# A two-layer and two-mixer block on one core: GpSimd's low parts of the weights in four operations instead of one

## The chip, the core and the metric

The kernel runs on one core of a Trainium2 chip. The metric is the device time of one execution in microseconds; several executions are timed, and the median counts.

## What is computed

The reference runs two models one after the other on a sequence of 512 tokens of width 1024, in float32. The first has two transformer layers with a context of 256 tokens (so 768 tokens in its first layer), the second two mixer layers. Cut to the matrix products and what stands between them:

```python
# first block, layer 0 (neighborhood attention) and layer 1 (sliding window attention)
u = modulate(rms_norm(h, g_mix), shift, scale)
q, k, v = split(u @ wqkv); y = attention(rms_norm(q), rms_norm(k), v) @ wo
h = h + gate * y
h = h + gate2 * (square(relu(modulate(rms_norm(h, g_mlp), shift2, scale2) @ w1)) @ w2)
# second block, layer 0: differential attention and mLSTM side by side; layer 1: gated spatial mixer
y = concat(diff_attention(hn @ w_in), mlstm_chunkwise(hn @ w_in)) @ w_out
h = h + rmsnorm(y, post_g)
y = (gelu(u) * (w_spatial @ rmsnorm(gelu(v))) * silu(z)) @ w_out     # u, v, z = hn @ w_in
h = h + rmsnorm(y, post_g)
```

## The kernel before

Every large product is made in three passes. A float32 operand is written as a high part, rounded to the matmul's fp32r format, and a low part, the rest. `mm3` (lines 274 to 278) issues three matmuls for each tile: high by high, low by high, high by low. So all weights must be split too. They stream from HBM in chunks of 128 partitions x 2048 columns into two slots of `w_raw` (m.raw). For each chunk, in a fixed order of chunks:

- SyncE issues the load once both parts of the chunk that had the slot before are made.
- ScalarE copies `w_raw` to `w_hi` (`split_hi`, line 239, or a line of the stage), once TensorE has used the slot's old high part.
- GpSimd subtracts: `w_lo` = `w_raw` - `w_hi`. It waits for ScalarE's count, makes one tensor_tensor of 2048 columns, and raises the count on which TensorE and SyncE wait. This is `split_lo` (line 242) in the MLP stages, and a line of the stage's own in the others: L1209 in the first attention stage, L1802 in the second, L2382 and L2385 in the differential attention, L2880 and L2883 in the mLSTM, L3495 in the last mixer.
- TensorE waits for the low part before the first matmul on the chunk.

The stages follow each other, each a block with its own program on every engine: first attention (`na_stage`), MLP, second attention (`swa_stage`), MLP, differential attention (`diff_stage`), mLSTM, last mixer (`odd_stage`). Each engine works through a fixed list of instructions; the waits between the lists are semaphore counts, and nothing is reordered at run time.

What VectorE does between the products matters here. At the start of a stage it makes the normalized input `u_lo`, in pairs of instructions per 128 channels: a scaling (L463) and a subtraction (L472, or L470 where there is no shift), with ScalarE's `u_hi` between them; TensorE waits for each 128 channels. In the attention stages it makes the softmax of one unit (a pair of heads or a head, and a block of queries) while TensorE scores the next one and works through projections. In `swa_stage` that is `maximum` (reductions L1952 and L1955, then L1960, a tiny operation on `stat`), the exponentials on ScalarE (L1846, L1849), and `normalise` (L1967 to L1973), whose `e` TensorE transposes (L2160). In `diff_stage` it is `maximum` (L2525, L2529), the exponentials (L2430), and `combine` (L2535 to L2540), whose `e` goes to TensorE at L2706; `low_y` (L2564) makes the low part of the attention's output between two such units. In `na_stage` the maxima end in L1364 and `e` is made in L1377 for TensorE's L1566.

GpSimd has one other kind of work: five additions of squares for each of six norms (L356).

Of the kernel before, what the change touches and what calls it, by code (L numbers as in the profile page):

```python
# [7 lines left out]
ALU = mybir.AluOpType  # L8
ACT = mybir.ActivationFunctionType
F32 = mybir.dt.float32  # L10
# [6 lines left out]
LAT = 512  # L17
# [10 lines left out]
CHUNK = 2048  # L28
# [212 lines left out]

def split_lo(pool, m, c, s, width=CHUNK):
    pool.wait_ge(m.hi_split, m.s0 + c + 1)
    pool.tensor_tensor(m.wl[:, s, 0:width], m.raw[:, s, 0:width], m.wh[:, s, 0:width].bitcast(F32),  # L244
                       ALU.subtract).then_inc(m.lo_split, 1)
# [810 lines left out]
def na_stage(nc, m):  # L1056
# [3 lines left out]
    with ExitStack() as ctx:  # L1060
# [92 lines left out]
        with nc.Block() as block:  # L1153
# [50 lines left out]
            @block.gpsimd  # L1204
            def _(pool):
                for n, f in enumerate(fills):
                    s = n % 2
                    pool.wait_ge(*chunk_hi.at(n + 1))
                    pool.tensor_tensor(m.wl[:, s, :], m.raw[:, s, :], m.wh[:, s, :].bitcast(F32),  # L1209
                                       ALU.subtract).then_inc(chunk_lo.sem)  # L1210
                split_lo(pool, m, 0, 0)
                after.add(pool)
# [432 lines left out]
def swa_stage(nc, m, rstd_u):  # L1645
# [3 lines left out]
    with ExitStack() as ctx:  # L1649
# [98 lines left out]
        with nc.Block() as block:  # L1748
# [49 lines left out]
            def _(pool):  # L1798
                for n, f in enumerate(fills):
                    s = slot[f]  # L1800
                    pool.wait_ge(*chunk_hi.at(n + 1))
                    pool.tensor_tensor(m.wl[:, s, :], m.raw[:, s, :], m.wh[:, s, :].bitcast(F32),  # L1802
                                       ALU.subtract).then_inc(chunk_lo.sem)
# [459 lines left out]
def diff_stage(nc, m, rstd_u):  # L2263
# [4 lines left out]
    with ExitStack() as ctx:  # L2268
# [77 lines left out]
        with nc.Block() as block:  # L2346
# [31 lines left out]
            def _(pool):  # L2378
                for n, f in enumerate(fills):
                    s = n % 2  # L2380
                    pool.wait_ge(*chunk_hi.at(n + 1))
                    pool.tensor_tensor(m.wl[:, s, :], m.raw[:, s, :], m.wh[:, s, :].bitcast(F32),  # L2382
                                       ALU.subtract).then_inc(chunk_lo.sem)
                pool.wait_ge(*m.ahead_hi.at(1))
                pool.tensor_tensor(m.wl[:, 0, :], m.raw[:, 0, :], m.wh[:, 0, :].bitcast(F32),  # L2385
                                   ALU.subtract).then_inc(m.ahead_lo.sem)
# [384 lines left out]
def mlstm_stage(nc, m):  # L2771
# [3 lines left out]
    with ExitStack() as ctx:  # L2775
# [82 lines left out]
        with nc.Block() as block:  # L2858
# [17 lines left out]
            def _(pool):  # L2876
                for n in range(1, len(fills)):
                    s = n % 2
                    pool.wait_ge(*chunk_hi.at(n))
                    pool.tensor_tensor(m.wl[:, s, :], m.raw[:, s, :], m.wh[:, s, :].bitcast(F32),  # L2880
                                       ALU.subtract).then_inc(chunk_lo.sem)
                pool.wait_ge(*m.ahead_hi.at(2))
                pool.tensor_tensor(m.wl[:, 0, :], m.raw[:, 0, :], m.wh[:, 0, :].bitcast(F32),  # L2883
                                   ALU.subtract).then_inc(m.ahead_lo.sem)
# [535 lines left out]
def odd_stage(nc, m, post0, out):  # L3420

    NC, G, GD, PRE = LAT // P, 8, 256, N_ADA + 3 * PAIRS + 32 + 3 * KV_HEADS + 32 + 24 + 20
    with ExitStack() as ctx:
# [50 lines left out]
        with nc.Block() as block:  # L3474
# [16 lines left out]
            def _(pool):  # L3491
                for n in range(1, len(fills)):
                    s = n % 2
                    pool.wait_ge(*chunk_hi.at(n))
                    pool.tensor_tensor(m.wl[:, s, :], m.raw[:, s, :], m.wh[:, s, :].bitcast(F32),  # L3495
                                       ALU.subtract).then_inc(chunk_lo.sem)
# [451 lines left out]
```

## Time and profile before

| what | value |
|---|---|
| three runs | 2996.72, 3002.36, 3004.58 us (median 3002.36) |
| the profiled execution | 2998.89 us |
| its span | 2996.9 us, mean granted TensorE clock 0.973 |
| TensorE busy | 2778.8 us, 93% |
| VectorE busy | 1433.9 us, 48% |
| ScalarE busy | 1096.4 us, 37% |
| GpSimd busy | 797.1 us, 27% |

The profiled execution took 3.5 us less than the median, which is within the spread of the three. The span is from the first to the last instruction; 2.0 us lie around it. A busy time counts an instruction from its start to its end as the profiler records them, so an instruction that stands still after its start counts as busy. In a timeline row the bracket at the end tells how long the engine had been idle and what released it.

### The profile page before, as it was taken

To read this page: it belongs to the slowest core of one execution; us is meant where nothing else is said; L and a number is where in the kernel's file an instruction comes from. 1 tells how busy PE (TensorE), PEld (TensorE's weight loads), DVE (VectorE), ACT (ScalarE), POOL (GpSimd) and SP (SyncE) were. 2 spreads that over 40 slices of the span, in tenths; PEclk is the share of its full clock that TensorE was granted. 3 is DMA by queue.
4 is the path that set the end of the run, shared out by engine and by line. 5 is a ranking of instruction groups with operands and counts; after the bars stand their busy time and mean duration, and the time that the engine had idled before them with its cause. 6 is when DMAs were issued, how large, how long until landed. Compare 5 with 4: busy or idle time off the path is not lost. (4 is left out here: it accounts for less than half of the span.)

```text
span 2996.9 us, 39763 instructions
## 1 busy us (share of the span) xinstructions
PE 2778.8 (93%) x16020; PEld 2253.5 (75%) x16020; DVE 1433.9 (48%) x2467; ACT 1096.4 (37%) x1844; POOL 797.1 (27%) x197
## 2 busy tenths in 40 slices
PE   5889999789999999899889999889998999899997
PEld 3777878668888887766657878667777888598886
DVE  4335344544333344556653344455556455605655
ACT  3444444442122222455542222334443434433222
POOL 1101111032222232211123434422331333243433
PEclk9999999999999999999999999999998999999999
DMA  6122323211112111122202222221211222122221
GB/s 228 57 101 106 125 98 112 83 43 56 70 56 70 56 57 51 57 85 85 95 32 85 86 96 98 73 71 57 71 60 61 76 80 71 58 87 96 90 93 56
DMA packets 54276, 238.91 MB, mean 80 GB/s; under 512 B 4212, under 2 KB 22132, under 8 KB 29944
## 3 DMA queue, kind: packets, MB, share of 16 engines
q1 hardware_dynamic: 54136, 236.94, 22.5%
q8 instruction: 100, 1.64, 0.2%
q14 instruction: 40, 0.33, 0.0%
HBM read 234.83 MB, written 2.10 MB: 79 GB/s over the span
## 5 line engine op out<-in xcount | busy, mean ns | idle before, releaser
L276 PE MATMUL bank<-u_hi,w_hi 128*128 128x512 f32 x1984 | 753.4, 380 | 55.9 <-DVE u_lo L472 22.9
L277 PE MATMUL bank<-u_lo,w_hi 128*128 128x512 f32 x1984 | 739.8, 373 | 0.0
L278 PE MATMUL bank<-u_hi,w_lo 128*128 128x512 f32 x1984 | 739.4, 373 | 0.0
L244 POOL TENSOR_TENSOR w_lo<-w_raw,w_hi 128x2048 fp32r<-128x2048 f32 x64 | 295.1, 4612 | 719.7 <-ACT w_hi L239 719.7
L276 PEld LDWEIGHTS bank<-u_hi,w_hi 128*128 128x128 f32 x1984 | 382.6, 193 | 137.0 <-issue 23.2
L277 PEld LDWEIGHTS bank<-u_lo,w_hi 128*128 128x128 f32 x1984 | 382.5, 193 | 63.5 <-issue 1.9
L278 PEld LDWEIGHTS bank<-u_hi,w_lo 128*128 128x128 f32 x1984 | 381.1, 192 | 64.8
L800 DVE SCALAR_TENSOR_TENSOR resid<-bank,mod,resid 128x512 f32<-128x512 f32 (+1 forms) x384 | 242.3, 659 | 171.5 <-PE bank L278 169.5
L276 PE MATMUL bank<-hid_hi,w_hi 128*128 128x512 f32 (+1 forms) x768 | 277.0, 361 | 3.8 <-DVE resid L800 3.8
L277 PE MATMUL bank<-hid_lo,w_hi 128*128 128x512 f32 (+1 forms) x768 | 274.1, 357 | 0.0
L278 PE MATMUL bank<-hid_hi,w_lo 128*128 128x512 f32 (+1 forms) x768 | 272.8, 355 | 0.0
L239 ACT ACTIVATE w_hi<-w_raw 128x2048 fp32r<-128x2048 f32 x64 | 122.7, 1917 | 309.1 <-PE bank L278 307.2
L787 DVE TENSOR_TENSOR square<-relu 128x768 f32<-128x768 f32 (+1 forms) x64 | 57.9, 905 | 364.2 <-ACT relu L693 364.0
L276 PE MATMUL bank<-w_hi,u_hi 128*128 128x256 f32 x752 | 215.0, 286 | 1.6 <-ACT qk_sq L1235 1.3
L277 PE MATMUL bank<-w_lo,u_hi 128*128 128x256 f32 x752 | 212.7, 283 | 0.0
L278 PE MATMUL bank<-w_hi,u_lo 128*128 128x256 f32 x752 | 212.7, 283 | 0.0
L3495 POOL TENSOR_TENSOR w_lo<-w_raw,w_hi 128x2048 fp32r<-128x2048 f32 x31 | 144.1, 4648 | 235.7 <-ACT w_hi L3508 235.7
L1209 POOL TENSOR_TENSOR w_lo<-w_raw,w_hi 128x2048 fp32r<-128x2048 f32 x16 | 73.1, 4569 | 465.9 <-ACT w_hi L1221 465.9
L276 PEld LDWEIGHTS bank<-hid_hi,w_hi 128*128 128x128 f32 x768 | 144.1, 188 | 34.6 <-DVE resid L800 10.4
L693 ACT ACTIVATE relu<-bank 128x768 f32<-128x768 f32 (+1 forms) x64 | 45.2, 706 | 323.2 <-PE bank L278 323.2
L278 PEld LDWEIGHTS bank<-hid_hi,w_lo 128*128 128x128 f32 x768 | 144.3, 188 | 22.5
L277 PEld LDWEIGHTS bank<-hid_lo,w_hi 128*128 128x128 f32 x768 | 144.7, 188 | 20.9
(374 smaller groups left out, 4635.7 us busy)
## 6 DMA issues: line engine op xcount, KB each, us to landing
w_raw<-stream SPq DMA_DIRECT2D x184, 1024.0 KB, 4.8
w_raw<-stream SPq DMA_DIRECT2D x44, 512.0 KB, 4.5
bias<-bias SPq DMA_DIRECT2D x8, 896.0 KB, 6.7
ada_more<-stream SPq DMA_DIRECT2D x4, 1024.0 KB, 11.6
resid<-h SPq DMA_DIRECT2D x1, 3072.0 KB, 10.4
out<-resid SPq DMA_DIRECT2D x8, 256.0 KB, 2.0
w_raw<-stream SPq DMA_DIRECT2D x4, 256.0 KB, 3.5
cos_sin<-cst SPq DMA_DIRECT2D x1, 512.0 KB, 8.3
```

Source lines behind the costliest of these rows:

```text
L239: act.activation(m.wh[:, s, 0:width], m.raw[:, s, 0:width], ACT.Copy).then_inc(m.hi_split, 1)
L244: pool.tensor_tensor(m.wl[:, s, 0:width], m.raw[:, s, 0:width], m.wh[:, s, 0:width].bitcast(F32), ALU.subtract).then_inc(m.lo_split, 1)
L276: pe.matmul(out, lh, rh, start=start, stop=False)
L277: pe.matmul(out, lh, rl, start=False, stop=False)
L278: return pe.matmul(out, ll, rh, start=False, stop=stop)
L693: act.activation(relu[:, par, t, :], m.lin[t][:, 0:tok], ACT.Relu).then_inc(*A.mark(f"e_{g}{t}"))
L787: dve.tensor_tensor(square[:, t, :], relu[:, par, t, :], relu[:, par, t, :], ALU.mult).then_inc(*D.mark(f"s_{g}{t}"))
L800: ins = dve.scalar_tensor_tensor(out=m.h[:, n, a:b], in0=m.lin[n % 2][:, a:b], scalar=m.mod[:, layer, 5, n, w:w + 1], in1=m.h[:, n, a:b], ...
L1209: pool.tensor_tensor(m.wl[:, s, :], m.raw[:, s, :], m.wh[:, s, :].bitcast(F32), ALU.subtract).then_inc(chunk_lo.sem)
L3495: pool.tensor_tensor(m.wl[:, s, :], m.raw[:, s, :], m.wh[:, s, :].bitcast(F32), ALU.subtract).then_inc(chunk_lo.sem)
```

## The change

A new function makes the low part of a chunk in pieces of LAT = 512 columns, with the same operation on each; all stages call it. The wait for ScalarE's count stays in front of the first piece, and the count for TensorE and SyncE is raised by the last piece alone. The 163 low parts of the program, each of 2048 columns, become 652 operations of 512 columns.

```diff
+def low_part(eng, m, s, width=CHUNK, piece=LAT):
+
+    for a in range(0, width, piece):
+        w = slice(a, min(a + piece, width))
+        ins = eng.tensor_tensor(m.wl[:, s, w], m.raw[:, s, w], m.wh[:, s, w].bitcast(F32), ALU.subtract)
+    return ins
+
+
 def split_lo(pool, m, c, s, width=CHUNK):
     pool.wait_ge(m.hi_split, m.s0 + c + 1)
-    pool.tensor_tensor(m.wl[:, s, 0:width], m.raw[:, s, 0:width], m.wh[:, s, 0:width].bitcast(F32),
-                       ALU.subtract).then_inc(m.lo_split, 1)
+    low_part(pool, m, s, width).then_inc(m.lo_split, 1)
...
                     pool.wait_ge(*chunk_hi.at(n + 1))
-                    pool.tensor_tensor(m.wl[:, s, :], m.raw[:, s, :], m.wh[:, s, :].bitcast(F32),
-                                       ALU.subtract).then_inc(chunk_lo.sem)
+                    low_part(pool, m, s).then_inc(chunk_lo.sem)
```

The last hunk stands for seven places with the same edit, in the five stages besides the MLPs. No other engine's program changes. GpSimd's own list in the second attention stage was this, before:

```order
L1797 UNCONDITIONAL_BRANCH
L1802 TENSOR_TENSOR w_lo<-w_raw,w_hi 128x2048 x11
L244 TENSOR_TENSOR w_lo<-w_raw,w_hi 128x2048
L356 TENSOR_TENSOR resid<-resid 128x2x256 x5
L1748 UNCONDITIONAL_BRANCH
```

With the change the same place reads:

```order
L1803 UNCONDITIONAL_BRANCH
L246 TENSOR_TENSOR w_lo<-w_raw,w_hi 128x512 x48
L363 TENSOR_TENSOR resid<-resid 128x2x256 x5
L1754 UNCONDITIONAL_BRANCH
```

Twelve low parts became 48 pieces, four in a row for each chunk, and the additions of squares still follow behind them.

## Rows read from the trace of the kernel before

**Rows 1.** The page's busy times and instructions of each engine.
```profile
PE 2778.8 (93%) x16020; PEld 2253.5 (75%) x16020; DVE 1433.9 (48%) x2467; ACT 1096.4 (37%) x1844; POOL 797.1 (27%) x197
```

**Rows 2.** Groups of GpSimd instructions: line, engine, operation, tiles, shapes, count; busy us, mean ns; idle before.
```profile
L244 POOL TENSOR_TENSOR w_lo<-w_raw,w_hi 128x2048 fp32r<-128x2048 f32 x64 | 295.1, 4612 | 719.7 <-ACT w_hi L239 719.7
...
L356 POOL TENSOR_TENSOR resid<-resid 128x512 f32<-128x512 f32 x20 | 25.9, 1293 | 23.3 <-ACT resid L349 21.0
```

**Rows 3.** TensorE's waits: who waited for whom, us in total, times, longest us.
```profile
PE bank L276 <- DVE u_lo L472: 22.9, 4, 9.6
PE bank L2706 <- DVE e L2540: 22.1, 9, 3.8
...
PE bank L2160 <- DVE e L1973: 16.7, 12, 3.7
...
PE bank L1566 <- DVE e L1377: 9.9, 6, 8.3
```

**Rows 4.** Timeline of the second attention stage: start us, us, engine, line, operation.
```profile
1456.86 4.59 POOL L1802 TENSOR_TENSOR w_lo<-w_raw,w_hi 128x2048 fp32r<-128x2048 f32 x1 [27.84 <-ACT w_hi L1814]
...
1458.71 2.76 DVE L1960 SCALAR_TENSOR_TENSOR stat<-stat 128x2 f32<-128x2 f32 x1
...
1465.59 0.90 PE L2160 MATMUL bank<-cst_sb,e 128*128 128x128 f32 x3 [2.42 <-DVE e L1973]
...
1466.96 0.16 DVE L1960 SCALAR_TENSOR_TENSOR stat<-stat 128x2 f32<-128x2 f32 x1
```

**Rows 5.** Timeline of the differential attention, around one low_y.
```profile
2059.89 4.63 POOL L2382 TENSOR_TENSOR w_lo<-w_raw,w_hi 128x2048 fp32r<-128x2048 f32 x1 [10.43 <-ACT w_hi L2396]
...
2060.36 4.70 DVE L2564 TENSOR_TENSOR y_lo<-o,y_hi 128x512 fp32r<-128x512 f32 x1 [3.30 <-ACT y_hi L2458]
...
2069.72 1.12 PE L2706 MATMUL bank<-cst_sb,e 128*128 128x128 f32 x4 [3.79 <-DVE e L2540]
```

**Rows 6.** Timeline of GpSimd and VectorE at the differential attention's start.
```profile
1939.45 4.51 POOL L2382 TENSOR_TENSOR w_lo<-w_raw,w_hi 128x2048 fp32r<-128x2048 f32 x1 [11.58 <-ACT w_hi L2396]
```
```profile
1943.92 4.97 POOL L2382 TENSOR_TENSOR w_lo<-w_raw,w_hi 128x2048 fp32r<-128x2048 f32 x1
```
```profile
1943.50 1.01 DVE L470 TENSOR_TENSOR u_lo<-z,u_hi 128x512 fp32r<-128x512 f32 x1 [9.63 <-ACT u_hi L447]
...
1944.43 5.01 DVE L463 SCALAR_TENSOR_TENSOR gate<-resid,vec_sb 128x512 f32<-128x512 f32 x1
```

**Rows 7.** Timeline at the last mixer's start, VectorE busy without a break.
```profile
2588.58 5.67 POOL L3495 TENSOR_TENSOR w_lo<-w_raw,w_hi 128x2048 fp32r<-128x2048 f32 x1 [7.89 <-ACT w_hi L3508]
```

**Rows 8.** Second attention stage's start: timeline; then busy us (PE, PEld, DVE, ACT, POOL), clock.
```profile
1196.10 4.50 POOL L1802 TENSOR_TENSOR w_lo<-w_raw,w_hi 128x2048 fp32r<-128x2048 f32 x1 [14.85 <-ACT w_hi L1814]
1196.67 4.48 DVE L472 SCALAR_TENSOR_TENSOR u_lo<-pt,mod,u_hi 128x512 fp32r<-128x512 f32 x1 [7.36 <-ACT u_hi L449]
...
1201.29 0.77 PE L276 MATMUL bank<-u_hi,w_hi 128*128 128x512 f32 x1 [7.16 <-DVE u_lo L472]
```
```profile
1201.30:1214.60 13.30, 13.29 (x48) 10.46 (x48) 13.30 (x26) 7.46 (x13) 0.00 (x0) 0.83 0.24 79
```

**Rows 9.** The stretch behind the wait of rows 4; columns as in the last of rows 8.
```profile
1465.30:1468.60 3.30, 3.02 (x18) 2.39 (x22) 1.79 (x7) 0.58 (x1) 0.00 (x0) 0.50 0.07 30
```

**Rows 10.** Timeline: two more held VectorE operations, at 98 and 1991 us.
```profile
98.38 3.55 DVE L1364 SCALAR_TENSOR_TENSOR stat<-stat 128x2 f32<-128x2 f32 x1
```
```profile
1990.99 4.25 DVE L2529 TENSOR_SCALAR stat<-stat 128x2 f32<-128x2 f32 x1
```

**Rows 11.** Timeline of TensorE in the mLSTM: the one matmul released by a low part.
```profile
2376.67 0.50 PE L276 MATMUL bank<-u_hi,w_hi 128*128 128x512 f32 x1 [0.28 <-POOL w_lo L2880]
```

**Rows 12.** Timeline of the second MLP: a low part, and the first matmul on its chunk.
```profile
1594.26 4.63 POOL L244 TENSOR_TENSOR w_lo<-w_raw,w_hi 128x2048 fp32r<-128x2048 f32 x1 [10.12 <-ACT w_hi L239]
...
1602.22 0.39 PE L276 MATMUL bank<-u_hi,w_hi 128*128 128x512 f32 x1
```

More of the change, by code:

```diff
@@ L1801, in _ @@
                     pool.wait_ge(*chunk_hi.at(n + 1))
-                    pool.tensor_tensor(m.wl[:, s, :], m.raw[:, s, :], m.wh[:, s, :].bitcast(F32),
-                                       ALU.subtract).then_inc(chunk_lo.sem)
+                    low_part(pool, m, s).then_inc(chunk_lo.sem)
                 split_lo(pool, m, 0, 0)
@@ L2381, in _ @@
                     pool.wait_ge(*chunk_hi.at(n + 1))
-                    pool.tensor_tensor(m.wl[:, s, :], m.raw[:, s, :], m.wh[:, s, :].bitcast(F32),
-                                       ALU.subtract).then_inc(chunk_lo.sem)
+                    low_part(pool, m, s).then_inc(chunk_lo.sem)
                 pool.wait_ge(*m.ahead_hi.at(1))
-                pool.tensor_tensor(m.wl[:, 0, :], m.raw[:, 0, :], m.wh[:, 0, :].bitcast(F32),
-                                   ALU.subtract).then_inc(m.ahead_lo.sem)
+                low_part(pool, m, 0).then_inc(m.ahead_lo.sem)
             @block.scalar
@@ L2879, in _ @@
                     pool.wait_ge(*chunk_hi.at(n))
-                    pool.tensor_tensor(m.wl[:, s, :], m.raw[:, s, :], m.wh[:, s, :].bitcast(F32),
-                                       ALU.subtract).then_inc(chunk_lo.sem)
+                    low_part(pool, m, s).then_inc(chunk_lo.sem)
                 pool.wait_ge(*m.ahead_hi.at(2))
-                pool.tensor_tensor(m.wl[:, 0, :], m.raw[:, 0, :], m.wh[:, 0, :].bitcast(F32),
-                                   ALU.subtract).then_inc(m.ahead_lo.sem)
+                low_part(pool, m, 0).then_inc(m.ahead_lo.sem)
                 post.add(pool)
@@ L3494, in _ @@
                     pool.wait_ge(*chunk_hi.at(n))
-                    pool.tensor_tensor(m.wl[:, s, :], m.raw[:, s, :], m.wh[:, s, :].bitcast(F32),
-                                       ALU.subtract).then_inc(chunk_lo.sem)
+                    low_part(pool, m, s).then_inc(chunk_lo.sem)
                 post1.add(pool)
```

## The prediction

> **What bounds the kernel now.** I read four views in this order. The page's busy times come first: TensorE is busy 2778.8 us of a 2996.9 us span, and no other engine comes near [rows 1]. So the end is set by TensorE's own work and the 218 us in which it stands idle. GpSimd is busy for 27%; its rate bounds nothing on average, and what the change does is decided by who waits at which moment. The waits of TensorE, read next, name VectorE most often: `u_lo` at the stages' starts, and `e`, the softmax, in the three attention stages [rows 3]. The timelines ahead of these waits, read third, show the thing on which this case turns. A VectorE operation on two columns, which takes 0.16 us a few microseconds later, takes 2.76 us, and it ends at 1461.47, 0.02 us after the low part that GpSimd had begun before it (1456.86 + 4.59 = 1461.45) [rows 4]. A subtraction of 512 columns takes 4.70 us and ends at 2065.06, 0.54 us behind GpSimd's end [rows 5]. So GpSimd's instruction holds back VectorE operations that read SBUF alone (all with two tensor inputs, some with one) until it ends; those that read PSUM run on. Most of the holds end while TensorE still has queued work. Last, the granted clock: behind a longer wait of TensorE it drops to 0.50, the 1.2 GHz level, for 3.3 us or more [rows 9].
>
> The Trainium skill states this hold as a rule (SBUF — State Buffer, the section on its two separate sides): the read and write ports that VectorE and GpSimd share are an exclusive lock, kept for the whole instruction, and the loser blocks fully. By that rule the length of one GpSimd instruction, not GpSimd's load, is what VectorE waits for; the rows agree (2.76 us for 0.16 us of work).
>
> **What the change costs.** A GpSimd operation of 512 columns takes 1293 ns, one of 2048 columns 4612 [rows 2]. Four of 512 take 5172 ns by these durations: +0.56 us for each low part, times 163 = +91 us of GpSimd work, spread over an engine that is idle for 2200 us. These durations overlap a little: two low parts that follow without a wait start 4.47 us apart though the first takes 4.51 [rows 6]. I take 1.25 us from piece to piece, and 5.0 to 5.2 us for the chunk.
>
> Whether VectorE gets its turn between two pieces is the heart of it. The trace has one place where low parts follow back to back: `u_lo` L470 is issued at 1943.50, the first low part ends at 1943.96, `u_lo` ends at 1944.51 (so it ran in between), and the second low part takes 4.97 us where the first took 4.51 [rows 6]. Then the next VectorE operation, issued at 1944.43, takes 5.01 us. So both take turns: a waiting VectorE operation goes first at the boundary, at about 0.4 us for GpSimd. Where VectorE has a queue without breaks, GpSimd's start costs it up to 1.06 us (5.67 against 4.61) [rows 7]. A low part in four pieces so takes 5.0 us with VectorE quiet and up to 5.0 + 4 x 1.06 = 9.3 us with VectorE dense.
>
> **Who waits longer for the low part.** TensorE and SyncE do. In the second MLP, the stage with the shortest lead, the low part ends at 1598.89 and the first matmul on it starts at 1602.22, 3.3 us later [rows 12]; the VectorE work there reads mostly PSUM, so +0.6 to +1 us is hidden. This is the pattern of all its rounds. One matmul of the mLSTM is released by a low part now [rows 11]; a VectorE operation of 0.7 us falls into that low part, so it starts 0.6 + 0.7 = 1.3 us later: **+1.3 us**.
>
> **The stages' starts.** In six of them VectorE makes scaling and `u_lo` in pairs without a break, and the first `u_lo` is held for 3.9 us, to GpSimd's end at 1200.60 [rows 8]. TensorE's 7.16 us wait looks like a prize, but VectorE has to yield the whole of GpSimd's time in any case: 4.5 - 0.57 = 3.9 us before, 5.2 - 0.57 = 4.6 us after, in four parts. What comes of it depends on what TensorE waits for. In the two MLPs the first low part was made a stage earlier, TensorE can start 3 us sooner on the first channels, but ends behind VectorE's last ones: I take -1 us each. In the first and second attention stage the first matmul needs the low part too; with turns it comes 1.5 us later, and from there TensorE runs without a gap (13.29 of 13.30 us busy [rows 8]), so that this passes through: +1.5 us each. The start at 1939 has both, -0.7 us; the last mixer's has VectorE's sum alone, +0.6 us. Together -2.0 + 3.0 - 0.7 + 0.6 = **+0.9 us**. Bounds: -6 us (each first `u_lo` a gain) and +8 us (the low part 4.3 us later at two gates).
>
> **The second attention stage.** Seven low parts start 1.85 us before L1960 (1458.71 - 1456.86), and each holds it for 2.6 us; behind three of them TensorE waits, 2.42, 2.42 and 3.73 us [rows 3, 4]. With pieces of 1.25 us the hold ends at 2.50 us: 0.65 us is left, and 1.95 us go. The later operations of this chain come after GpSimd's end. 3 x 1.95 = **-5.9 us**. The waits left are 0.5, 0.5 and 1.8 us.
>
> **The differential attention.** Three times `low_y` is issued 0.47 us behind a low part, is held for 4.0 us, and TensorE waits 3.8 us for the `e` behind it [rows 5]. The first boundary frees it after 0.8 us. But L2529, which GpSimd can hold for 4.1 us as another place shows [rows 10], now comes while a third or fourth piece runs and is held for 0 to 1.25 us, and `e` may be once more. The gain is 4.0 - 0.8 = 3.2 us at most and 3.2 - 2 x 1.25 = 0.7 at least. I take one further hold: 2.0 us, 3 x 2.0 = **-6.0 us**. Held operations of the same stage stand before two smaller waits (the L2529 at 1991 us is one): **-2.5 us** of their 3.0.
>
> **The first attention stage.** L1364 is held for 3.4 us at 98 us, and TensorE waits 8.3 us behind it [rows 3, 10]. 0.3 us is left of this hold, and one further hold is likely: **-1.8 us**. The other holds of this stage and of the mLSTM, and seven of 3.6 us in the last mixer, have TensorE work as cover; I take 0.
>
> **The clock.** Behind each of the six waits of these two stages TensorE ran at half clock for 3.3 us or more, and was busy for 3.0 us of them [rows 9]; full clock would halve that, 1.5 us. Behind a wait of 0.5 us I expect no fall, behind 1.8 us perhaps: between 0 and 6 x 1.5 = 9 us. I take three whole and three halves: **-6.7 us**.
>
> The sum: -5.9 - 6.0 - 2.5 - 1.8 - 6.7 + 0.9 + 1.3 = -20.7 us. These stages go on alternating between TensorE and VectorE behind each place, so some of it comes back as the next wait; I give back a quarter, which is a choice: **-15.5 us**. Against the profiled 2998.9 us that is 2983.4; the median of the runs shown is 3.5 us above it, so 3002.4 - 15.5 = **2987 us**.
>
> **The rivals.** *The holds shrink, the time doesn't* (20%). TensorE's waits move from `e` to the next thing, a score not ready or a bank not read. For it: four of the seven holds in the second attention stage already cost nothing. Against: the waits follow the held operation directly. A third of the stage gains of 16.2 us, no clock, and the costs: -5.4 + 2.2 = -3 us, 2999 us.
>
> *No turn between the pieces* (12%). If a piece's successor takes the ports before a waiting VectorE operation does, each hold lasts 0.5 us longer instead of shorter. Some eleven holds are on the path, and six starts: +5 to +8 us, 3009 us. Only one boundary in the trace speaks against it, and there GpSimd's second instruction had its own semaphore wait. The Trainium skill has a rule on this side (GPSIMD Engine Reference, Instruction dispatch): completion does not hold back the next GpSimd instruction; each of its eight cores goes on as soon as its own share is done. By it the pieces might run into each other with the ports never free; the boundary at 1943.96, where `u_lo` ended 0.55 us into the second low part, does not look so.
>
> *Slower: the low part becomes the gate at the stages' starts* (10%). The place is the first projection of three stages, where TensorE's first matmul needs `u_lo` and `w_lo` [rows 8]. VectorE is dense there, and four pieces at 1.25 + 1.06 us end 9.3 us behind the start, 4.8 us later than now. It decides from the point where GpSimd loses two VectorE operations at each boundary and not one, and the idle time ahead also keeps the clock low for longer: 3 x 4.8 + 3 x 1.5 = +19 us. If further holds also eat the gains in the attention stages but for 3 us, this gives +16 us, 3018 us.
>
> **How the numbers follow.** My forecast has 58%, with its own range from 2976 (the upper gain of 3.2 us three times, all of the clock, nothing given back: -26) to 2996 (the lower gains, no clock). The rivals have 20, 12 and 10%. A measurement of this kernel can tell about 0.3% from no change, 9 us: faster is below 2993.4, slower above 3011.4. Of my forecast 5 points lie within; so does the first rival, and the second but for 2 points. Faster 0.53, same 0.35, slower 0.12. The range leaves out the slower rival and the outermost gains: 2974 to 3006.
>
> **What would show it.** GpSimd: 652 operations of about 1.29 us, some 0.4 to 1 us longer beside a dense VectorE, busy time near 890 us. VectorE: no hold above 1.4 us, L1960 at 0.8 us instead of 2.76, L2564 below 2 us; its busy time falls. TensorE: the waits for `e` L1973 and L2540 fall from 38.8 us together to about 24, and the stretches behind the first are granted the full clock; waits for `u_lo` stay much the same in sum. Wrong would be: holds of 4 us still there (no turns), a wait of TensorE for `w_lo` at three starts (the gate), or short holds with unchanged waits of TensorE (absorbed).

## The result and the profile after

The changed kernel takes 2974.26 us in the median of four runs (2970.42 to 2980.46), beside 3003.47 us for four runs of the kernel before. The ratio is 0.9907, with a 95% interval from 0.9893 to 0.9920: 28 us faster. In a second job it was 0.9906 (0.9887 to 0.9925). The forecast was 2987 us, 15.5 us faster than the median shown; the range reached down to 2974 and holds the result by 0.3 us only, which is luck; the forecast's own narrower range ended at 2976. The sign and the mechanism were right, the size was half of what came.

The profiled execution took 2970.42 us, its span is 2968.4 us, with a mean granted TensorE clock of 0.978 (0.973 before). The page's busy times and instructions of each engine:

```profile
PE 2766.2 (93%) x16020; PEld 2242.0 (76%) x16020; DVE 1343.0 (45%) x2467; ACT 1096.8 (37%) x1844; POOL 901.3 (30%) x686
```

Against [rows 1], GpSimd is 104 us busier and VectorE 91 us less busy, though it executes the same 2467 instructions. Since these are the same instructions, the 91 us are, on balance, holds that are gone. TensorE executes the same 16020 matmuls in 12.6 us less busy time, and stands still for 2968.4 - 2766.2 = 202.2 us where it was 2996.9 - 2778.8 = 218.1. So this execution's gain of 28.5 us is **15.9 us less standstill and 12.6 us less busy time**, and the second part I put down to the clock: where two stretches of the same matmuls have the same granted clock, their busy times agree (539.86 and 539.87 us in the first attention stage, both at 0.97, in the tables below). This split is used below for all runs.

GpSimd's groups (line, engine, operation, tiles, shapes, count, busy us, mean ns, idle before), for [rows 2]:

```profile
L246 POOL TENSOR_TENSOR w_lo<-w_raw,w_hi 128x512 fp32r<-128x512 f32 x652 | 856.8, 1346 | 2009.1 <-ACT w_hi L239 684.7 <-ACT w_hi L1227 455.6 <-ACT w_hi L1819 253.5
```

TensorE's waits (who waited for whom, us in total, times, longest us), for [rows 3]:

```profile
PE bank L283 <- POOL w_lo L246: 22.0, 3, 10.8
PE bank L496 <- DMA w_raw<-stream: 20.1, 5, 14.7
PE bank L1549 <- DVE y_lo L1397: 12.8, 16, 2.2
PE bank L2709 <- DVE e L2543: 12.3, 6, 3.6
PE bank L2165 <- DVE e L1978: 12.1, 12, 2.3
...
PE bank L1572 <- DVE e L1383: 7.7, 6, 6.1
...
PE bank L283 <- DVE u_lo L479: 4.6, 5, 1.6
```

The waits for `e` in the three attention stages fell from 9.9, 16.7 and 22.1 us to 7.7, 12.1 and 12.3. At the starts the name has changed: `u_lo` L472 had 22.9 us, `u_lo` L479 now has 4.6, and 22.0 us stand under `w_lo`. The line numbers are higher because the new function stands above: L1965 was L1960, L1978 L1973, L2165 L2160, L2567 L2564, L2532 L2529, L2543 L2540, L2709 L2706, L479 L472, L470 L463, L283 L276.

The second attention stage, at the place of [rows 4] (start us, us, engine, line, operation, tiles, count, idle before):

```profile
1453.66 5.02 POOL L246 TENSOR_TENSOR w_lo<-w_raw,w_hi 128x512 fp32r<-128x512 f32 x4 [27.39 <-ACT w_hi L1819]
...
1455.52 0.69 DVE L1965 SCALAR_TENSOR_TENSOR stat<-stat 128x2 f32<-128x2 f32 x1
...
1460.94 0.55 PE L2165 MATMUL bank<-cst_sb,e 128*128 128x128 f32 x3 [0.96 <-DVE e L1978]
```

The tiny operation starts 1.86 us behind the low part, as before, and takes 0.69 us instead of 2.76: it ends in the middle of the low part, and TensorE waits 0.96 us instead of 2.42. The differential attention, at the place of [rows 5]:

```profile
2045.51 5.50 POOL L246 TENSOR_TENSOR w_lo<-w_raw,w_hi 128x512 fp32r<-128x512 f32 x4 [9.78 <-ACT w_hi L2399]
2045.98 1.38 DVE L2567 TENSOR_TENSOR y_lo<-o,y_hi 128x512 fp32r<-128x512 f32 x1 [3.31 <-ACT y_hi L2461]
...
2048.62 1.17 DVE L2532 TENSOR_SCALAR stat<-stat 128x2 f32<-128x2 f32 x1
...
2052.22 0.75 DVE L2543 SCALAR_TENSOR_TENSOR e<-e,stat 128x512 f32<-128x512 f32 x1
...
2053.03 0.65 PE L2709 MATMUL bank<-cst_sb,e 128*128 128x128 f32 x4 [1.47 <-DVE e L2543]
```

`y_lo` takes 1.38 us instead of 4.70. L2532, 0.17 us of work on two columns with one tensor as input, is held for 1.0 us by the third piece, and is the one further hold that the prediction allowed for; TensorE waits 1.47 us instead of 3.79. Over the whole trace no VectorE instruction is longer than the shortest of its kind by more than 1.14 us; before, 41 were longer by over 1.4 us, up to 4.45.

The start of the second attention stage, at the place of [rows 8]:

```profile
1192.95 6.29 POOL L246 TENSOR_TENSOR w_lo<-w_raw,w_hi 128x512 fp32r<-128x512 f32 x4 [14.53 <-ACT w_hi L1819]
1193.52 1.26 DVE L479 SCALAR_TENSOR_TENSOR u_lo<-pt,mod,u_hi 128x512 fp32r<-128x512 f32 x1 [7.38 <-ACT u_hi L456]
1194.69 1.75 DVE L470 SCALAR_TENSOR_TENSOR pt<-resid,gsc,rstd_first 128x512 f32<-128x512 f32 x1
1196.37 1.75 DVE L479 SCALAR_TENSOR_TENSOR u_lo<-pt,mod,u_hi 128x512 fp32r<-128x512 f32 x1
...
1199.29 0.80 PE L283 MATMUL bank<-u_hi,w_hi 128*128 128x512 f32 x1 [10.03 <-POOL w_lo L246]
...
1215.41 0.58 PE L283 MATMUL bank<-u_hi,w_hi 128*128 128x256 f32 x1 [2.33 <-ACT x L1827]
```

Here VectorE is dense, and the two engines take strict turns: each VectorE operation of 0.75 us takes 1.75, and the low part takes 6.29 us instead of 4.50. TensorE's wait of 10.0 us is 2.9 us longer than before and is now a wait for the low part. Only part of the 2.9 us is the low part's: ahead of the wait TensorE works through ten rows of products with constants, which both kernels have, and they took 6.23 us before, partly at half clock, and take 4.53 us here. TensorE is done with them 1.7 us earlier against GpSimd's start.

Where the time went is read by stage. The same stretches of the program, from one matmul to the same matmul, are cut out of both traces: first attention; first MLP with the start of the second attention; second attention; second MLP with the start of the differential attention; differential attention; then the mLSTM. The columns after the length are busy us and instructions of PE, PEld, DVE, ACT and POOL, then the granted clock. Before:

```profile
67.00:661.40 594.40, 539.86 (x4025) 435.11 (x4025) 265.03 (x604) 269.53 (x552) 88.85 (x23) 0.97 0.25 91
661.40:1222.60 561.20, 547.41 (x3047) 473.67 (x3046) 224.70 (x348) 130.73 (x122) 152.15 (x36) 0.99 0.17 59
1222.60:1585.70 363.10, 328.54 (x2157) 235.58 (x2156) 210.16 (x490) 180.77 (x427) 61.50 (x17) 0.97 0.21 70
1585.70:1955.40 369.70, 353.61 (x1502) 282.05 (x1501) 156.00 (x202) 108.00 (x109) 149.89 (x36) 0.98 0.26 91
1955.40:2339.70 384.30, 348.29 (x1791) 279.69 (x1790) 216.36 (x416) 155.34 (x294) 105.84 (x23) 0.95 0.20 65
2339.70:2604.20 264.50, 250.46 (x1231) 199.14 (x1230) 142.21 (x153) 103.66 (x129) 86.64 (x22) 0.97 0.20 72
```

After:

```profile
66.40:658.50 592.10, 539.87 (x4024) 434.59 (x4024) 247.25 (x604) 269.69 (x552) 98.34 (x75) 0.97 0.25 92
658.50:1219.30 560.80, 546.32 (x3047) 473.42 (x3047) 224.51 (x348) 130.78 (x122) 166.99 (x130) 0.98 0.17 59
1219.30:1576.90 357.60, 326.89 (x2157) 233.43 (x2156) 193.41 (x490) 181.12 (x427) 70.35 (x54) 0.98 0.20 72
1576.90:1945.60 368.70, 353.00 (x1502) 281.33 (x1501) 159.31 (x200) 107.25 (x108) 164.09 (x129) 0.99 0.26 90
1945.60:2311.10 365.50, 339.08 (x1791) 272.06 (x1790) 197.96 (x419) 156.10 (x296) 120.50 (x92) 0.98 0.21 70
2311.10:2575.70 264.60, 249.58 (x1232) 198.50 (x1231) 129.00 (x153) 103.47 (x129) 98.61 (x73) 0.98 0.20 72
```

Length less PE busy is TensorE's standstill. It changes by -2.3, +0.7, -3.9, -0.4, -9.6 and +1.0 us; ahead of the first stretch it falls by 1.4 us, and in the last mixer it stays the same. The differential attention is 18.8 us shorter: 9.6 us of standstill and 9.2 us of busy time, at a clock of 0.98 instead of 0.95. Two thirds of this execution's gain is made in that one stage.

### The profile page after: what moved, and what is told of

Its sections match the earlier page's. It is cut to its first block and busy times, and to the rows that moved or that the text cites. A ratio compares the mean times of both kernels' runs of the same rounds, so it can differ in the third digit from the quotient of the medians.

```text
span 2968.4 us, 40252 instructions
## 1 busy us (share of the span) xinstructions
PE 2766.2 (93%) x16020; PEld 2242.0 (76%) x16020; DVE 1343.0 (45%) x2467; ACT 1096.8 (37%) x1844; POOL 901.3 (30%) x686
## 5 line engine op out<-in xcount | busy, mean ns | idle before, releaser
L246 POOL TENSOR_TENSOR w_lo<-w_raw,w_hi 128x512 fp32r<-128x512 f32 x652 | 856.8, 1346 | 2009.1 <-ACT w_hi L239 684.7
L283 PE MATMUL bank<-u_hi,w_hi 128*128 128x512 f32 x1984 | 751.0, 379 | 57.0 <-POOL w_lo L246 22.0
L283 PEld LDWEIGHTS bank<-u_hi,w_hi 128*128 128x128 f32 x1984 | 379.8, 191 | 139.0 <-issue 35.1
L283 PE MATMUL bank<-hid_hi,w_hi 128*128 128x512 f32 (+1 forms) x768 | 276.6, 360 | 3.7 <-DVE resid L807 3.7
L283 PE MATMUL bank<-w_hi,u_hi 128*128 128x256 f32 x752 | 215.0, 286 | 1.6 <-ACT qk_sq L1241 1.3
L283 PEld LDWEIGHTS bank<-hid_hi,w_hi 128*128 128x128 f32 x768 | 144.1, 188 | 34.1 <-DVE resid L807 10.4
L283 PEld LDWEIGHTS bank<-w_hi,u_hi 128*128 128x128 f32 x752 | 144.2, 192 | 7.3 <-issue 6.2
L284 PEld LDWEIGHTS bank<-w_lo,u_hi 128*128 128x128 f32 x752 | 144.2, 192 | 0.4 <-issue 0.2
```

The lines of the kernel that those rows point to most:

```text
L246: ins = eng.tensor_tensor(m.wl[:, s, w], m.raw[:, s, w], m.wh[:, s, w].bitcast(F32), ALU.subtract)
L283: pe.matmul(out, lh, rh, start=start, stop=False)
L284: pe.matmul(out, lh, rl, start=False, stop=False)
```

## Experiments

Twelve runs were made, two of them repeats of the change and of the kernel before, each in five rounds in turns with the kernel before. "Time" is the ratio to before times its median; its 95% interval is 3 to 6 us to either side. Standstill is span less PE busy in the one profiled execution.

| run | ratio (95% interval) | time, us | standstill, us | PE busy, us |
|---|---|---|---|---|
| before, first and second trace | 1; 1.0007 (0.9997, 1.0018) | 0, +2 | 218.1, 218.2 | 2778.8, 2782.3 |
| the change, first and second job | 0.9907; 0.9906 (0.9887, 0.9925) | -28, -28 | 202.2, 201.1 | 2766.2, 2776.8 |
| two pieces of 1024 | 0.9946 (0.9932, 0.9960) | -16 | 205.1 | 2781.0 |
| eight pieces of 256 | 0.9898 (0.9882, 0.9915) | -31 | 198.4 | 2772.3 |
| four, differential attention alone | 0.9950 (0.9936, 0.9964) | -15 | 207.7 | 2772.9 |
| four, all but differential attention | 0.9992 (0.9982, 1.0002) | -2 | 212.9 | 2778.6 |
| four, two first low parts whole | 0.9927 (0.9909, 0.9946) | -22 | 203.4 | 2776.5 |
| before, 14 products in three waits | 1.0058 (1.0040, 1.0076) | +17 | 207.2 | 2807.7 |
| before, 3 products in three waits | 0.9976 (0.9965, 0.9988) | -7 | 208.3 | 2787.3 |
| nearly no low parts | 0.9769 (0.9749, 0.9789) | -69 | 166.6 | 2764.2 |
| sizes by stage | 0.9897 (0.9882, 0.9912) | -31 | 197.5 | 2777.5 |
| sizes by stage and products | 0.9887 (0.9870, 0.9903) | -34 | 184.0 | 2781.6 |

**The size of a piece.** If a hold ends at the next boundary, the length of a piece is the length of a hold. One default was changed, for two pieces and then for eight:

```diff
-def low_part(eng, m, s, width=CHUNK, piece=LAT):
+def low_part(eng, m, s, width=CHUNK, piece=2 * LAT):
```

> Two pieces of 1024 columns (about 2.4 us each) in all stages. Theory (VectorE gets its turn at every boundary, and the time comes from shorter holds before waits for e): no hold above 2.5 us; the tiny L1960 (L1965), which comes 1.85 us behind the low part's start, is held some 0.6 us, as with four pieces; y_lo is held 2.0 us where it was 4.0, and a further hold of up to 2.4 us may follow. Against before: -12 to -20 us, some 60% of the change's -29. Rival (the time comes from something that every cut brings at once, a GpSimd that never runs 4.6 us in one go): -25 us or more already. Rival (the holds matter only once they are near 1 us, shorter than the lead TensorE has): under -6 us.

```diff
-def low_part(eng, m, s, width=CHUNK, piece=LAT):
+def low_part(eng, m, s, width=CHUNK, piece=LAT // 2):
```

> Eight pieces of 256 columns in all stages, by the line through 1293 ns for 512 and 4612 ns for 2048 columns some 0.74 us each, 5.6 us for a low part. Theory: holds of 0.75 us at most, so a few tenths more off each wait for e than with four, but w_lo 0.5 to 2 us later at the starts of the first and second attention stage: -26 to -33 us against before, that is, within 4 us of the change. Rival (VectorE's and GpSimd's start costs grow with the number of boundaries and take it back): -20 us or less, with a wait for w_lo of 14 us or more at the second attention's start.

Two pieces gave -16 us, eight -31 us. The place of [rows 5] with two pieces:

```profile
2052.09 5.22 POOL L246 TENSOR_TENSOR w_lo<-w_raw,w_hi 128x1024 fp32r<-128x1024 f32 x2 [10.24 <-ACT w_hi L2399]
2052.57 2.48 DVE L2567 TENSOR_TENSOR y_lo<-o,y_hi 128x512 fp32r<-128x512 f32 x1 [3.31 <-ACT y_hi L2461]
...
2056.31 1.03 DVE L2532 TENSOR_SCALAR stat<-stat 128x2 f32<-128x2 f32 x1
...
2060.57 0.66 PE L2709 MATMUL bank<-cst_sb,e 128*128 128x128 f32 x4 [2.44 <-DVE e L2543]
```

And with eight:

```profile
2050.87 6.28 POOL L246 TENSOR_TENSOR w_lo<-w_raw,w_hi 128x256 fp32r<-128x256 f32 x8 [9.23 <-ACT w_hi L2399]
2051.34 0.82 DVE L2567 TENSOR_TENSOR y_lo<-o,y_hi 128x512 fp32r<-128x512 f32 x1 [3.31 <-ACT y_hi L2461]
2052.09 0.68 DVE L2528 CUSTOM_DVE_ANT_0 s<-bank,causal 128x512 f32<-128x512 f32 x1
...
2057.76 0.66 PE L2709 MATMUL bank<-cst_sb,e 128*128 128x128 f32 x4 [0.84 <-DVE e L2543]
```

`y_lo` takes 4.70, 2.48, 1.38 and 0.82 us with one, two, four and eight pieces, and TensorE's wait behind it is 3.79, 2.44, 1.47 and 0.84 us. Each halving of the piece shortens the hold, and the wait follows. This settles the mechanism: VectorE gets its turn at every boundary. No hold of the whole trace is above 0.63 us with eight pieces. This also refutes both rivals of the first run (nothing yet with two pieces, or all of it), and eight pieces cost nothing that could be measured, though the low part takes 6.28 us. With one, two, four and eight pieces, all waits for `e` of the differential attention together are 22.1, 16.5, 12.3 and 9.7 us. In the second attention stage they are 16.7, 12.0, 12.1 and 12.0 us: there two pieces already give all that can be had.

**Where the time comes from.** Four pieces in the differential attention alone, and everywhere else:

```diff
-def low_part(eng, m, s, width=CHUNK, piece=LAT):
+def low_part(eng, m, s, width=CHUNK, piece=CHUNK):
...
-                    low_part(pool, m, s).then_inc(chunk_lo.sem)
+                    low_part(pool, m, s, piece=LAT).then_inc(chunk_lo.sem)
```

> Four pieces in the differential attention alone, one of 2048 columns in all other stages. Theory (holds and clock of the differential attention carry most of it): -18 to -22 us against before, the waits for e L2543 12.3 us as in the change, those for e in the second attention 16.7 us as before. Rival (the stages share it in proportion to my prediction, 12.5 of 20.7): -15 us or less, and the rest elsewhere.

```diff
-                    low_part(pool, m, s).then_inc(chunk_lo.sem)
+                    low_part(pool, m, s, piece=CHUNK).then_inc(chunk_lo.sem)
```

> Four pieces in all stages but the differential attention. Theory: -7 to -10 us against before, nearly all from the second attention and the start of the first; together with the run that cuts the differential attention alone it adds up to the change's -29 within 4 us. Rival (the parts of the program lean on each other, by clock or by DMA timing): the two don't add up, the gap is over 6 us.

Both expectations missed: -15 us is less than the 18 to 22 of the first, -2 less than the 7 to 10 of the second. The times don't add up: -15 and -2 are 11 us short of -28. The standstill does: 218.1 - 207.7 = 10.4 and 218.1 - 212.9 = 5.2 us make 15.6, where the change has 15.9 and, in its second trace, 17.0. So what the waits give is additive, and what is missing is clock. To see whether the first measurement had been lucky, the change ran once more:

> The changed kernel itself, once more, on the chip of the next three, because the part in the differential attention (-15 us) and the part outside it (-2.4 us) add up to only -17 us of -29. Theory (the two add up, and the first measurement of the whole lay at one end of what runs scatter): -20 to -26 us here. Rival (the parts help each other): -28 us or more again.

It gave -28 us again, so the theory of a lucky measurement falls. The second trace's busy line:

```profile
PE 2776.8 (93%) x16020; PEld 2247.2 (75%) x16020; DVE 1342.6 (45%) x2467; ACT 1096.0 (37%) x1844; POOL 901.1 (30%) x686
```

Its span is 2977.9 us. The standstill is within 1.1 us of the first trace, the busy time of the same matmuls is 10.6 us longer. A third of that, and half of the 9.5 us between the two spans, lies in the opening, ahead of the first attention stage. The same stretch in the first trace and in the second, columns as in the tables by stage:

```profile
31.00:41.00 10.00, 6.75 (x84) 4.20 (x84) 3.89 (x13) 3.77 (x5) 0.00 (x0) 1.00 0.45 147
```

```profile
31.00:45.00 14.00, 12.12 (x85) 6.89 (x84) 3.14 (x12) 2.38 (x4) 0.00 (x0) 1.00 0.23 84
```

TensorE is busy for 6.75 us with 84 matmuls in the one and for 12.12 us with 85 in the other, and both are shown with a clock of 1.00. The second trace has 1.00 without a break up to 57 us. I take it that half clock is missing from its record there, so its mean clock of 0.979 is too high; this is inferred, not shown. The traces of the runs with two pieces, with 3 products and with sizes by stage have the same longer opening (71.4 to 71.7 us against 66.6 to 67.4 in the other traces). The kernel before, run against itself, has its standstill again too:

> The kernel before itself, for a second trace of it. Theory (TensorE's standstill belongs to the program and is the same in each execution; the time at half clock is not, and makes the scatter): standstill within 1.5 us of 218.9, the time at half clock anywhere from 145 to 175 us, the ratio of times 1.000 within 0.002. Rival (the first trace of before was an odd one, and part of the change's gain is only that): standstill under 214 us, or half-clock time near the change's 128 us.

```profile
PE 2782.3 (93%) x16020; PEld 2254.9 (75%) x16020; DVE 1428.9 (48%) x2467; ACT 1096.4 (37%) x1844; POOL 797.1 (27%) x197
```

The standstill is 218.2 us, 0.1 from the first trace; the busy time differs by 3.5 us. The mean clock of 0.971 means 2 x 0.029 x 3000.5 = 174 us at half clock, beside 162 us in the first trace and 131 us in the change's first; the 125 us of the change's second lacks the opening. So the standstill belongs to the program, and the busy time scatters between executions of one program by 4 to 11 us.

Why the clock's part is larger for the whole change (-28 + 16.5 = some -12 us) than for its two halves (-5 and +3) stays open, but the differential attention shows where some of it lies. Four traces have this stage in four pieces, all with a standstill of 26.4 to 26.5 us, and it took 365.5 us in the change's first trace, 368.5 in its second, and 371.0 both in the run with this stage alone in pieces and in the one with two first low parts whole, at clocks of 0.98, 0.97, 0.96 and 0.96. So the 9.2 us of busy time that this stage saved in the first trace is the best of four; against the same trace of before the others saved 6.3, 3.7 and 3.7 us. The gap between the times is 11 us, and the intervals of the ratios together allow some 6 us of scatter in it.

**The clock by itself.** In the kernel before, TensorE was given products with constants inside the three long waits for `e`, written into a bank that the transposes overwrite. The holds and the ends of the waits stay as they are.

```diff
                 def turn(G):
                     i, t = units[G]
+                    if G in (11, 19, 27):
+                        pe.wait_ge(*max_parts.at(G + 1))
+                        keep_busy(pe, m, banks(G)[:, 1, :], 14)
```

> The kernel before, with low parts whole, and 14 products of 512 columns with constants (3.0 us of TensorE work whose result the transposes overwrite) put into the three 3.8 us waits for e behind y_lo in the differential attention, so that TensorE does not stand still there; the holds and the wait's end stay. Theory (a part of the gain of the change is the clock behind these waits, in the change's trace 1.2, 2.3 and 1.2 us): full clock behind the three places, -3 to -6 us against before. Rival (the clock falls for what lies further back, or the gain is from the holds alone): 0 to -1 us, or up to +1.5 us where the products end behind e.

```profile
2063.99 12.28 PE L284 MATMUL bank<-cst_sb 128*128 128x512 f32 x28 [0.40 <-DVE stat L2525]
```

It was 17 us slower, by my mistake, and so says nothing on the clock: 14 products are recorded as 28 rows and take 12.28 us, 0.88 us each, not 0.21. With three of them:

> As the run with 14 products in each of the three waits, but with 3. One such product with float32 constants took 0.85 us there (28 rows in 12.28 us for 14 products), not the 0.21 us I had counted, so 14 ended 8 us behind e; 3 take 2.6 us and end before it. The holds and the ends of the waits stay. Theory (what the change gains beyond its 16 us less standstill of TensorE is clock, and part of that lies behind these waits): full clock behind the three places, -3 to -6 us against before. Rival (no clock is lost for these waits): 0 to -1 us.

It was 7 us faster than before (ratio 0.9976, 0.9965 to 0.9988), the upper end of what was expected and a little more. Three stretches of 24 us behind these waits, columns as above; in the kernel before:

```profile
2066.00:2090.00 24.00, 18.65 (x81) 14.16 (x82) 17.48 (x34) 10.55 (x24) 4.61 (x1) 0.93 0.29 88
2141.00:2165.00 24.00, 20.22 (x91) 16.39 (x90) 16.66 (x32) 8.85 (x21) 7.25 (x2) 0.86 0.16 44
2222.00:2246.00 24.00, 18.86 (x87) 14.22 (x86) 17.71 (x33) 10.16 (x23) 7.85 (x2) 0.93 0.13 44
```

And with three products:

```profile
2066.00:2090.00 24.00, 22.40 (x103) 16.59 (x101) 18.50 (x33) 9.64 (x23) 9.22 (x2) 1.00 0.16 44
2141.00:2165.00 24.00, 23.06 (x110) 16.99 (x109) 15.80 (x29) 11.60 (x25) 6.11 (x2) 1.00 0.16 44
2222.00:2246.00 24.00, 22.41 (x104) 16.18 (x104) 17.54 (x32) 11.33 (x25) 8.61 (x2) 1.00 0.13 44
```

In the first rows the clock is 0.93, 0.86 and 0.93, that is 2 x 24 x (0.07 + 0.14 + 0.07) = 13.4 us at 1.2 GHz, which costs half of it, 6.7 us. In the second it is 1.00 throughout, and 7 us are gone though no hold is shorter. So these three waits cost their own 11 us and 7 us of clock behind them. In the change's first trace the stretches behind the same three waits have a clock of 1.00 too.

**The starts of the attention stages.** The first low part of the first and of the second attention stage was left whole:

```diff
-                    low_part(pool, m, s).then_inc(chunk_lo.sem)
+                    low_part(pool, m, s, piece=LAT if n else CHUNK).then_inc(chunk_lo.sem)
```

> Four pieces everywhere but in the first low part of the first and of the second attention stage, which is one operation of 2048 columns as before. Theory (in pieces it comes 1.5 to 1.8 us later there, and TensorE waits for it): 2 to 3 us less than the change in the same job, the wait at the second attention's start back at 7.2 us from 10.0. Rival (VectorE's sum of scalings and subtractions sets the start, and takes back what the low part gives): within 1 us of the change.

```profile
1194.45 4.50 POOL L246 TENSOR_TENSOR w_lo<-w_raw,w_hi 128x2048 fp32r<-128x2048 f32 x1 [14.60 <-ACT w_hi L1819]
...
1199.64 0.77 PE L283 MATMUL bank<-u_hi,w_hi 128*128 128x512 f32 x1 [8.95 <-DVE u_lo L479]
...
1217.11 0.58 PE L283 MATMUL bank<-u_hi,w_hi 128*128 128x256 f32 x1 [4.74 <-ACT x L1827]
```

The theory falls: there is no gain. From GpSimd's start to the first matmul it is 1199.64 - 1194.45 = 5.19 us with the low part whole and 1199.29 - 1192.95 = 6.34 us in pieces, 1.15 us later. But to the next projection it is 22.66 us whole and 22.46 us in pieces. What TensorE loses at its first matmul it has back by the last channel, because the last `u_lo` sets the pace, and VectorE yields the same GpSimd work in either form; the wait for `x` behind it only becomes shorter (2.33 for 4.74 us). The standstill was 1.2 to 2.3 us longer than the change's. The median was 8 us above the change's in the same job; the intervals overlap, and what is more than the standstill is clock.

**What is left.** All low parts but the first two compute 16 of each 512 columns, so that GpSimd holds nearly nothing; the output lacks the low parts of most weights.

```diff
+        w = slice(a, min(a + min(piece, step), width))
```

> The low parts leave out all but 16 of each 512 columns (the first two chunks of the program are whole), so GpSimd has almost no work and holds nothing. It shows what is left to gain. Theory (VectorE has to yield the whole of GpSimd's time at the six starts of stages, and holds of up to 1.3 us stay in the change): the starts give about 3 us each beyond the change, the rest 2 to 6 us, so -42 to -55 us against before. Rival (the starts' waits are made by VectorE's own 16 to 24 operations): -30 to -35 us, little more than the change.

It was 69 us faster, more than either theory gave. The standstill is 166.6 us, 35 us under the change's, so GpSimd's subtractions still cost that much on the path. VectorE's busy time falls by another 111 us, to 1232.1. Shorter holds don't reach that: with eight pieces, none above 0.63 us, the standstill was still 198.4 us. Some of what is left is likely VectorE giving up time to GpSimd in dense stretches, the same in any number of pieces: TensorE's waits for `e` in the differential attention fall from 12.3 to 6.1 us. But this run also takes away the low part's own 4.5 to 6.3 us between ScalarE's copy and TensorE's first matmul on a chunk, and so frees the slots for the loads sooner: TensorE's waits for loads (`w_raw<-stream`) fall from 20.1 to 15.1 us. The runs don't separate the two.

**A combined kernel.** Sizes by stage, `2 * LAT` in the first two attention stages and `LAT // 2` in the differential one:

```diff
-def low_part(eng, m, s, width=CHUNK, piece=LAT):
+def low_part(eng, m, s, width=CHUNK, piece=CHUNK):
...
+                    low_part(pool, m, s, piece=2 * LAT).then_inc(chunk_lo.sem)
...
+                    low_part(pool, m, s, piece=LAT // 2).then_inc(chunk_lo.sem)
```

> The pieces by stage, as the traces so far rank them by TensorE's standstill: two pieces in the first and second attention stage, eight of 256 columns in the differential attention, one whole part elsewhere. Adding up the stages' standstill of the runs that had these sizes gives 194.5 us, against 218.9 before and 203.1 in the change. Theory (the stages' standstill adds up; the clock comes on top, some -5 to -12 us): -29 to -36 us against before, the median under the change's. Rival (what one stage saves is lost at the next stage's start): standstill of 200 us or more, no better than the change.

It gave -31 us and a standstill of 197.5 us, 3.6 to 4.7 us under the change's two traces but not the 8.6 expected. (The expectation counted gaps between matmul records, which gives 0.8 us more than span less busy.) It can't be told from the change by time. Last, eight pieces in the differential attention, four in the other two attention stages, whole low parts elsewhere, and products in long waits:

```diff
-                keep_busy(pe, m, lin.out(0), 5)
+                keep_busy(pe, m, lin.out(0), 10)
...
+                    if G in (30, 31):
+                        pe.wait_ge(*max_parts.at(G + 1))
+                        keep_busy(pe, m, banks(G)[:, 1, :], 3 if G == 30 else 2)
```

> What the runs point to, together: four pieces in the first and second attention stage, eight in the differential attention, whole parts elsewhere; and products with constants where TensorE waits long: 10 instead of 5 at the starts of the second and the differential attention, 3 and 2 in the last two waits for e of the differential attention. Theory (clock bought with work in waits comes on top of shorter holds): standstill under 190 us (some 9 us of it now filled), half-clock time under 120 us, -33 to -38 us against before, clear of the change's -28. Rival (what the clock gives at one place is taken by the next half-clock stretch, and the starts are paced by VectorE): -27 to -31 us, no better than the change.

The median is 2967.61 us (2965.77 to 2967.93) beside 3000.09, ratio 0.9887 (0.9870 to 0.9903): -34 us, the best of the kernels that make all low parts, with every run below every run of the change (2970.42 and up). The interval of the ratio still overlaps with the change's, so "better than the change by some 6 us" is likely and not proved. The standstill of 184.0 us looks lower than it is, since the added products fill some of it: they are 30 rows, so 15 products of 0.88 us, 13.2 us in all, and with them taken out the standstill is 197.2 us, that of the sizes by stage. The time at half clock, 2 x 0.021 x 2965.6 = 125 us, is not under the 120 expected. So what the products bought is not shown by this run.

## Why the prediction was right, and where its sizes failed

**The hold, and the turn between pieces: right.** "A waiting VectorE operation goes first at the boundary" was taken from one boundary, and holds at all of them. The predicted L1960 at 0.8 us is 0.69, L2564 below 2 us is 1.38, no hold above 1.4 us is 1.14 at most. The waits for `e` of the second and the differential attention, predicted to fall from 38.8 us to about 24, fell to 24.4. The Trainium skill's rule (SBUF — State Buffer, its two separate sides) that the lock is held for a whole instruction agrees, with 4.70, 2.48, 1.38 and 0.82 us for pieces of 2048, 1024, 512 and 256 columns. The Trainium skill also states that completion does not hold back the next GpSimd instruction (GPSIMD Engine Reference, Instruction dispatch). What the rival without turns made of that, ports that are never free between two pieces, is seen nowhere in these traces.

**The differential attention: right in its waits.** Predicted were 6.0 + 2.5 = 8.5 us less waiting; the stage's standstill fell by 9.6 us. Its start, predicted at -0.7 us, lies in the stretch before, which changed by -0.4 us. The wait behind `y_lo` shrank by 2.3 us where I took 2.0, with exactly one further hold of 1.0 us.

**The second attention stage: 5.9 us predicted, 3.9 to 4.6 measured.** L1960 ends 2.06 us earlier against GpSimd's start, as worked out (1.95), but TensorE's wait shrank by 2.42 - 0.96 = 1.46 us. The step that failed is that all of a hold's gain reaches the wait: here 0.6 us of it did not. The experiments say why more can't be had: the waits for `e` of this stage stay at 12.0 us with eight pieces and also with nearly no low parts, so what remains of them is no hold.

**The first attention stage: right.** Predicted -1.8 us, standstill -2.3 us.

**The starts: wrong for the two gates.** The step "it comes 1.5 us later, and from there TensorE runs without a gap, so that this passes through" failed, twice 1.5 us. The window of [rows 8] has TensorE busy for 13.29 of 13.30 us, but that is no proof that TensorE is the bound: behind it the next wait, for `x`, was 4.17 us and gives the difference back. From GpSimd's start to the next projection it was 22.66 us before and is 22.46 now. That the stretch with this start still has 0.7 us more standstill goes with the products ahead of it, which end 1.7 us earlier; the stretch itself is 0.4 us shorter. The opening, where the other gate lies, shows no 1.5 us more standstill either, but 1.4 us less. The row that I had not looked at, before:

```profile
1218.76 0.39 PE L276 MATMUL bank<-u_hi,w_hi 128*128 128x256 f32 x1 [4.17 <-ACT x L1822]
```

The prediction had named a wait for `w_lo` at three starts as a sign against itself. It came at two of them (20.9 of the 22.0 us under `w_lo`; the rest is the mLSTM's) and cost nothing. So the low part did become the gate, and the slower rival failed in what it made of that. Even at the 9.3 us that I feared it costs little: with eight pieces it took 8.69 us at this start, the next projection came 22.21 us after GpSimd's start, and that kernel was among the fastest.

```profile
1195.10 8.69 POOL L246 TENSOR_TENSOR w_lo<-w_raw,w_hi 128x256 fp32r<-128x256 f32 x8 [14.56 <-ACT w_hi L1819]
```

What the starts of the MLPs and of the last mixer gave, predicted within 1 us each, is too small to be told apart.

**The mLSTM: right.** Its one wait for `w_lo` [rows 11] grew from 0.28 to 1.14 us, the stage's standstill by 1.0 us; predicted was +1.3.

**Giving back a quarter: wrong.** Without clock and without giving back, the terms sum to -14.0 us; the standstill fell by 15.9 and 17.0 us in the two traces. Nothing came back as a next wait. That -14.0 is so near is partly two errors that cancel: the +3.0 us of the two gates did not come, and the second attention gave 1.3 to 2.0 us less than its term. The quarter cost 3.5 us of the prediction's waits.

**The clock: undersized.** Predicted were 6.7 us, 5.0 after giving back; measured about 12 by the medians, with a scatter of several us from execution to execution, and 7 of them by the run with 3 products, behind the three waits of the differential attention alone. The step that failed is "three whole and three halves" of 1.5 us: for those three I took 2.3 us. Half-clock time there was up to 6.7 us behind one wait, not 3.3 as in the single stretch that I had read [rows 9], and with a wait of 1.5 us left the clock did not fall at all. In the second attention the clock gave less than the 4.5 us I took: busy time there fell by 1.7 us.

Together: -16.5 us of standstill for -10.5, and -12 us of clock for -5. Of the rivals, the first (holds shrink, time doesn't) is refuted by the stage rows, the second by the lengths of `y_lo`, the third by the starts, where the gate came and the time did not.

## What to carry to other kernels

When two engines exclude each other for whole instructions, cut the instructions of the one whose results are ready well before their use: the other's hold is one piece long, and the cost (here 104 us of busy time on an engine with 2200 us of idle time) lands where it is covered. Cut most finely in the stage whose waits still shrink with the piece (here the differential attention; in the second attention two pieces gave all), and don't fear for a start that another engine's last operation sets. Split a trace's gain into standstill (span less busy) and busy time of the same matmuls: the first repeats within about 1 us, the second goes with the clock and scatters, so take it from more than one trace; and a wait's price on TensorE is the wait and the half-clock stretch behind it; read that stretch at each wait, not at one.

## What the runs showed of the hardware that was not expected

- VectorE and GpSimd, both dense, take strict turns: each operation of 0.75 us takes 1.75 us beside pieces of 512 columns. An operation on 2 columns waits as long for a piece (1.0 us for L2532) as one on 512 does.
- The three products in three waits, 7.9 us of useless work, made the kernel 7 us faster.
- One product of 128x128 by 128x512 with float32 constants took 0.88 us and is recorded as two rows, against 0.23 us from one fp32r product to the next in `mm3`.
- TensorE's standstill differed by 0.1 us between two executions of the kernel before and by 1.1 us between two of the change, while the busy time of the same matmuls differed by 3.5 and 10.6 us.
- In the opening of the change's two traces, 85 matmuls took 12.12 us in one and 84 took 6.75 us in the other, both under a shown clock of 1.00. That the slower one lacks half clock in its record is inferred.
